# RWKV-7 scan on Trainium2: level products merged in pairs, state and masked products split over array quarters, second state decay on GpSimd

## What is computed

```python
def step(state, inp):
    r_t, w_t, k_t, v_t, kk_t, a_t = inp
    sa = jnp.einsum('bhvk,bhk->bhv', state, -kk_t)
    state = (state * w_t[:, :, None, :] + sa[..., None] * (kk_t * a_t)[:, :, None, :]
             + v_t[..., None] * k_t[:, :, None, :])
    return state, jnp.einsum('bhvk,bhk->bhv', state, r_t)
```

## Time and profile before

| | |
|---|---|
| Median of 3 runs | 2628.55 us (2627.21 to 2631.51) |
| The profiled execution's own time | 2627.98 us |
| Its span | 2626.2 us |
| Busy PE, DVE, ACT, POOL | 2399.8, 1562.1, 1080.5, 775.4 us |
| Mean granted clock | 0.968 |
| Matmul records | 22291 |

### The profile page before, as it was taken

The page is one execution under the profiler, slowest core; times in us unless marked ns, Lnnn a source line. Parts: engine busy times, 40 slices in busy tenths (PEclk is TensorE's granted clock), DMA queues, the critical chain, the costliest instruction groups (busy, mean ns, idle before and its releaser), DMA issues. The chain is left out here.

```text
span 2626.2 us, 53374 instructions
## 1 busy us (share of the span) xinstructions
PE 2399.8 (91%) x22291; PEld 1864.5 (71%) x22291; DVE 1562.1 (59%) x2402; ACT 1080.5 (41%) x1951; POOL 775.4 (30%) x511
## 2 busy tenths in 40 slices
PE   5799999999997899999989799998998996999997
PEld 2488887788886888888878666666876884555554
DVE  3544458976663445555377566666885886544433
ACT  4311123343442566656465455553122221544443
POOL 1122244545451455444213200001300000444443
PEclk8999999999998999999999999999998997999998
DMA  8522224344435123332044611104755446899994
GB/s 343 210 81 80 80 89 156 119 149 153 157 119 186 55 74 86 95 100 73 22 153 118 161 33 34 29 12 162 237 158 212 151 148 234 318 359 347 353 322 113
DMA packets 196291, 399.28 MB, mean 152 GB/s; under 512 B 38698, under 2 KB 104010, under 8 KB 182994
## 3 DMA queue, kind: packets, MB, share of 16 engines
q1 hardware_dynamic: 173876, 322.58, 36.2%
q0 software_dynamic: 12960, 41.82, 6.0%
q10 hardware_dynamic: 9216, 31.46, 3.0%
HBM read 294.57 MB, written 106.48 MB: 153 GB/s over the span
## 5 line engine op out<-in xcount | busy, mean ns | idle before, releaser
L99 PE MATMUL ps_in<-h_t_low,w_in_high 128*128 128x512 f32 x960 | 378.7, 394 | 2.1 <-PEq L79 2.1
L100 PE MATMUL ps_in<-h_t_high,w_in_low 128*128 128x512 f32 x960 | 373.9, 389 | 0.0
L101 PE MATMUL ps_in<-h_t_high,w_in_high 128*128 128x512 f32 x960 | 373.8, 389 | 0.0
L99 PEld LDWEIGHTS ps_in<-h_t_low,w_in_high 128*128 128x128 f32 x960 | 180.2, 188 | 44.5 <-issue 5.6
L1275 POOL TENSOR_TENSOR wkv_levels<-wkv_nt,level_mask 128x1024 f32<-128x1024 f32 x60 | 140.5, 2359 | 230.0 <-ACT wkv_nt L1220 230.0
L101 PEld LDWEIGHTS ps_in<-h_t_high,w_in_high 128*128 128x128 f32 x960 | 180.2, 188 | 38.0
L100 PEld LDWEIGHTS ps_in<-h_t_high,w_in_low 128*128 128x128 f32 x960 | 180.3, 188 | 35.7
L607 ACT COPY p_row<-ps_in 128x512 f32<-128x512 f32 x72 | 42.4, 588 | 293.4 <-PE ps_in L101 256.3
L3078 PE MATMUL ps_xy<-w_tile,hidden_turned 128*128 128x512 f32 x272 | 123.6, 597 | 16.4 <-DMA w_tile<-in_w 15.0
L498 POOL CAST w_in_high<-w_in_tile 128x1024 fp32r<-128x1024 f32 x39 | 45.7, 1171 | 299.3 <-PE ps_in L101 297.2
L705 DVE TENSOR_SCALAR p_mixed<-p_row,mu_centre 128x1537 f32<-128x1537 f32 x24 | 35.3, 1473 | 148.0 <-ACT p_row L607 147.8
(11 more groups left out here) (432 smaller groups left out, 6221.0 us busy)
## 6 DMA issues: line engine op xcount, KB each, us to landing
merged_t<-in_w SPq DMA_DIRECT2D x36, 1024.0 KB, 11.2
w_tile<-in_w SPq DMA_DIRECT2D x34, 1024.0 KB, 15.4
w_now<-in_w SPq DMA_DIRECT2D x30, 1024.0 KB, 15.8
w_ada_tile<-in_w_ada SPq DMA_DIRECT2D x12, 2048.0 KB, 9.2
wkv_in<-wkv_out SPq DMA_DIRECT2D x24, 1024.0 KB, 3.9
w_in_tile<-in_w_in SPq DMA_DIRECT2D x40, 512.0 KB, 3.6
p_t<-p_mixed ACTq DMA_DIRECT2D x24, 512.0 KB, 2.7
gates<-p_mixed ACTq DMA_DIRECT2D x16, 768.0 KB, 4.6
```

The source lines that it names most:

```text
L99: nc.tensor.matmul(out, w[0], x[1], start=start, stop=False)
L100: nc.tensor.matmul(out, w[1], x[0], start=False, stop=False)
L101: return nc.tensor.matmul(out, w[0], x[0], start=False, stop=stop)
```

## The change

1. `level_z` and `level_xz` make 16 products of 128 rows by 64 columns of weights with 64 moving columns, where they made 32 of 64 by 64 with 32. For this `x` gets a second copy of its shape: half `c` of the partitions holds values in place `c` and zeros in place 1 - c. `xt_over` becomes `xt_wide`, laid out likewise; ACT fills it with four copies of 64x256 (`widen`) instead of two, and reads it alone. `turned` makes two transposes of 64x512 instead of one of 128x512.
2. `from_state` and `mask_v` write each 128 columns as two products of 64 columns, `half(a)` of the weights to half `a` of the output: 32 products on four quarters instead of 16.
3. The PSUM tile `LV` has its axes exchanged, so that the first results of a level lie in one bank and the second in the other; `half_product` writes the second bank alone.
4. `decay_again` goes from ACT to POOL, as four operations of 128x256, ahead of `level(j + 2, 0)` in a pass. `next_state` is two operations of 128x256 on DVE, a wait for them, and one of 128x512.
5. Beta and kappa have two buffers instead of three: `load_bk(j + 3)` stands behind `load_ar(j + 3)` in SP's stream and waits for the turning of tile j + 1.

```diff
-        AR, BK, LB = 3, 3, 3
+        AR, BK, LB = 3, 2, 3
-        x = s.sb("wkv_x", [P, 2, 2 * H, BLK])
+        x = s.sb("wkv_x", [P, 2, 2, 2 * H, BLK])
-        xt_over = s.sb("wkv_xt_over", [P, H, BLK])
+        xt_wide = s.sb("wkv_xt_wide", [P, 2, 2, H, BLK])
...
-                if j + 3 < N:
-                    load_bk(j + 3)
...
                 if j + 3 < N:
                     load_ar(j + 3)
+                    load_bk(j + 3)
                 store(j, 1)
...
+                        for a in range(2):
+                            mm = nc.tensor.matmul(G[half(a), r, CH * hh(g, f):CH * hh(g, f) + CH], lbm[half(r), i % LB, 2 * d + c, slot(c, g, f), half(a)],
+                                                  uv[half(r), i % 2, c, d, 2 * f + g], start=True, stop=True)
...
-                for d, f, c, b in level_tiles:
+                for d, f, b in column_halves:
                     h = H * d + RF * b + f
-                    mm = nc.tensor.matmul(LV[half(b), c, 0, RF * d + f], lev[half(c), l, h], x[half(c), i % 2, h], start=True, stop=True)
+                    mm = nc.tensor.matmul(LV[half(b), 0, :, RF * d + f], lev[:, l, h], x[:, i % 2, :, h], start=True, stop=True)
...
-                for d, f, c, b in level_tiles:
-                    right = xt[half(c), i % 2, H * d + RF * b + f] if b == c else xt_over[half(b), RF * d + f]
-                    mm = nc.tensor.matmul(LV[half(c), b, 1, RF * d + f], z[half(b), c, RF * d + f], right, start=True, stop=True)
+                for d, f, c in column_halves:
+                    mm = nc.tensor.matmul(LV[half(c), 1, :, RF * d + f], z[:, c, RF * d + f], xt_wide[:, c, :, RF * d + f], start=True, stop=True)
...
-                    for g in range(2):
-                        mm = nc.tensor.matmul(Q[:, g, d, CH * f:CH * f + CH], ar[half(g), i % AR, d, f, pair(c)], s0[half(g), c, f],
+                    for g, a in quarters:
+                        mm = nc.tensor.matmul(Q[half(a), g, d, CH * f:CH * f + CH], ar[half(g), i % AR, d, f, pair(c)][:, half(a)], s0[half(g), c, f],
                                               start=(n == 0), stop=True, skip_group_check=True)
...
                 for b in range(2):
-                    ins = nc.scalar.copy(xt_over[half(b)].rearrange("p (d f) t -> p d (f t)", d=2), by_side(xt[half(1 - b), i % 2])[:, :, b])
+                    for c in range(2):
+                        ins = nc.scalar.copy(xt_wide[half(b), c, b].rearrange("p (d f) t -> p d (f t)", d=2), by_side(xt[half(c), i % 2])[:, :, b])
...
+                pool.wait_ge(m["s0_ready"], 2 * i + k + 1)
+                for d in range(2):
+                    c = chunk(k, d)
+                    ins = nc.gpsimd.tensor_tensor(s1[:, 1 - c], s0[:, c], decay(i, k, d).to_broadcast([P, RF, CH]), ALU.mult)
+                ins.then_inc(m["s1_ready"], 1)
...
             for j in range(-2, N):
+                if j >= 0:
+                    decay_again(j, 0)
+                    decay_again(j, 1)
                 if j + 2 < N:
                     level(j + 2, 0)
...
-                return nc.vector.transpose(flat(dst), flat(src))
+                for c in range(2):
+                    ins = nc.vector.transpose(flat(dst[half(c), c]), flat(src[half(c)]))
+                return ins
...
-                        for f in range(RF):
-                            ins = nc.vector.scalar_tensor_tensor(out=s0[:, 1 - c, f], in0=S[:, c, CH * f:CH * f + CH], scalar=decay(i, k, d, f),
-                                                                 in1=s1[:, 1 - c, f], op0=ALU.mult, op1=ALU.add)
-                    ins.then_inc(m["s0_ready"], 1)
+                        ins = nc.vector.tensor_tensor(s0[:, 1 - c], S[:, c].rearrange("p (f t) -> p f t", f=RF), decay(i, k, d).to_broadcast([P, RF, CH]), ALU.mult)
+                    ins.then_inc(m["s0_part"], 1)
+                    dve.wait_ge(m["s0_part"], 2 * i + k + 1 - int(i >= RUNS[1][0]))
+                    nc.vector.tensor_tensor(s0[:], s0[:], s1[:], ALU.add).then_inc(m["s0_ready"], 1)
...
+            for c in range(2):
+                nc.vector.memset(x[half(c), :, 1 - c], 0.0).then_inc(m["zeros"], 1)
+                nc.vector.memset(xt_wide[half(c), :, 1 - c], 0.0).then_inc(m["zeros"], 1)
```

60 lines of the change are left out of this document (27 added, 33 removed).

## The result

The changed kernel takes 2659.13 us (median of 4 runs, 2657.02 to 2659.66) against 2629.82 for the kernel before on the same chip: a ratio of 1.0111, 95% interval 1.0093 to 1.0128. The forecast was 2623, its range ended at 2640. The profiled execution took 2657.02 us, 29.04 more than that of before.

What follows compares the result with a forecast made beforehand. TensorE's program order was taken to bound the scan. 2627.98 us + 1 for the instructions - 7 for stalls + 1 for the lower clock = 2623 us, range 2609 to 2640.

Steps and rivals of the forecast that it cites:

- What bounds the kernel: Scan: TensorE's program order, 31.46 of a quiet tile's 33.94 us, with the other engines filling its shadow.
- the prices on TensorE: Scan: state and masked products from 1.93 to 1.07 us, level products 1.05, half_product's single bank uncharged; 3.44 saved a tile.
- (b): State and masked products: quarters do not overlap, groups stay at 1.93 or 1.98 us; 2642 us, chance 0.10.
- (e): Level products: 128-row weight loads do not overlap, 4.4 us a product group; 2950 us, chance 0.01.
- The helpers: VectorE's turns take 1.30 us, +0.59 five times a tile; ScalarE's widen 1.66, +0.84 four times.
- The walk: One scan tile in three stretches, ending at products, level_z(·,4), next second masked product: 34.1 us; together +1 without stalls.
- Rival (a): Scan: walk too kind to the helpers, joints between instructions cost; tile 34.8 us, 2638 us, chance 0.19.
- Two beta/kappa buffers: SP's load waits for an earlier turning, lands in 4.9 us, before its data are wanted; nothing charged.
- Stalls: Inside TensorE's groups: four tenths of the 17 us go, swallowed by its longer waits; -7 us.
- Rival (c): TensorE in the scan: fewer records also mean fewer stalls, 14 instead of 7 us go; 2612 us, chance 0.16.
- More idling brings the clock down more often: TensorE's clock in the scan: more time at the lower level, +1 us, between 0 and +8.
- State decay: POOL and VectorE in the scan: costs nothing as long as s1 is there; cover 0.2 us.

Runs made afterwards that it cites:

- e6: Kernel before with only two beta/kappa buffers and the load's new place: 2663.34 us, 1.0121 of the kernel before.
- e1: Changed kernel with the beta/kappa load issued later, behind the next pass's first level product: 2632.57 us, 0.9987 of the kernel before.
- e5: Kernel before with only the split state and masked products: 2658.82 us, 1.0103 of the kernel before.
- e3: Changed kernel without the merge of the level products (64x64 products, one transpose a turn, copy_over): 2667.68 us, 1.0125 of the kernel before.
- e11: Changed kernel with the late beta/kappa load and both masked products whole: 2624.83 us, 0.9969 of the kernel before.
- h4: Changed kernel with late beta/kappa load, only level_z merged, first masked product whole, 64 more records before the first tile: 2619.37 us, 0.9959 of the kernel before.
- e10: Kernel before with half of the alpha/rho load moved behind the next pass's first level product: 2621.77 us, 0.9959 of the kernel before.
- e7: Kernel before with only decay_again on POOL and next_state in three operations: 2634.53 us, 1.0016 of the kernel before.
- the four shifts: Four late-load variants of the changed kernel with 32, 64 or 96 more records before the first tile, tiles unchanged: 0.9959 to 1.0025 of the kernel before.
- h1: Changed kernel with late beta/kappa load, first masked product whole, 64 more records before the first tile: 2639.41 us, 1.0025 of the kernel before.
- h3: Changed kernel with late beta/kappa load, only level_z merged, first masked product whole, 32 more records before the first tile: 2637.49 us, 1.0022 of the kernel before.
- f2: Changed kernel with late beta/kappa load, only level_z merged, first masked product whole, half of alpha/rho late too: 2636.07 us, 0.9982 of the kernel before.
- f4: Kernel before, three buffers, with beta/kappa and half of alpha/rho loaded behind the next pass's first level product: 2635.06 us, 0.9984 of the kernel before.

## Why the prediction failed, step by step

**What bounds the kernel; the prices on TensorE.** Right. State and masked products take 1.09 (forecast 1.07), level products 1.08 (1.05), so rivals (b) and (e) are out. The merged products' records follow each other 34 ns apart. `half_product` writes one bank in 0.68 us, as `cross_product` does.

**The helpers.** Right in size but for one addition. Timeline of DVE, changed kernel, end of one tile and beginning of the next:

```profile
1120.05 2.25 DVE L1376 TENSOR_TENSOR wkv_state_decayed<-wkv_state_decayed,wkv_state_decayed_twice 128x512 f32<-128x512 f32 x1
...
1136.52 1.43 DVE L1322 STREAM_TRANSPOSE wkv_x<-wkv_xt 64x512 f32<-64x512 f32 x2
```

Timelines of ACT, then of POOL, in the later of the two tiles:

```profile
1129.59 1.64 ACT L1185 COPY wkv_xt_wide<-wkv_xt 64x256 f32<-64x256 f32 x4
```

```profile
1137.09 1.23 POOL L1266 TENSOR_TENSOR wkv_state_decayed_twice<-wkv_state_decayed,p_end 128x256 f32<-128x256 f32 x2
```

A turn 1.43 (forecast 1.30), `widen` 1.64 (1.66), POOL's pair 1.23 (1.4), `next_state` 0.76 + 0.69 (1.6). The addition in the first row takes 2.25, of which more below. The state product that needs its result starts at 1132.13, ten microseconds after its end, so here it costs nothing.

**The walk.** Right: 34.3 us without stalls against 34.1. Stretch 1 took 12.0 (12.3), stretch 2 14.29 (13.9), stretch 3 8.08 (7.9). Rival (a) asked for 34.6 or more and did not come. So +1 us for the instructions themselves was sound, and the other 28 are elsewhere.

**"Two beta/kappa buffers: ... its data are wanted ... such a load lands in 4.9 us".** This is the step that failed. It asked whether the load comes in time, and it does. It did not ask what the load does while it lands. Before, it was issued in the middle of a pass; now it is issued beside the store at the end, so that masked, cross and level products run 5 to 8 us behind it. e6 prices the move alone at +1.2%, e1 its undoing at -1.2%. What it does shows in the packets: TensorE's next block of instructions starts behind the load's first 512 KB, up to 4.2 us after the border before instead of 1.2. The store behind it, which I had looked at, kept no engine waiting. The step isn't the only one that failed: e5 loses 1.0% with every load in its old place, and that belongs to the next term.

**"Stalls ... I take four tenths of the 17 us as gone: -7".** The second failed step, wrong in sign: +13.3. I had treated the stalls as evenly strewn, so that more waiting would swallow them. They stand at block borders, worst behind a load and where 128 records take less than the 3.3 to 3.9 us from one block to the next. The split put 128 more records into a tile, 96 of them into the seam between two passes, which was dense already. Rival (c) had the one half of it that is true, that fewer records mean fewer stalls: e3 against the changed kernel, 63.5 to 29.6. The other half, that the split undoes this at its place, is e5 (58.5).

**"More idling brings the clock down more often: +1, between 0 and +8".** Mis-sized: 27.3 us more at the lower clock, some 12 us of time by the estimate above. With next to no stalls (e11) the eleven tiles run at 1.00. But the lower clock doesn't go by the sum of the stalls: h4 has 30.2 us of short ones and none of it, e10 14.3 us and 44.4 of it. What brings it down is not shown here.

**State decay: nothing.** Right (e7).

**What would show it.** The last mark that I had named, a lower clock for more than twice the time now, came true in the eleven tiles (47.8 us against 20.5), though not over the whole scan (65 against 39); I had not said which. A mark for the stalls themselves was missing.

**What stays open.** That TensorE stalls at the borders of its instruction blocks is shown by the counts, the four shifts and the packets, and so is that a load delays a block. Open is when TensorE asks for one. After a wait of TensorE the packet can start before the border before is reached, up to 0.9 us in the changed kernel, and a dense block there passes without a stall; I have no rule that forecasts this, and mine failed in h1, h3 and h4. Open too is what brings the clock down.

## What to carry to other kernels

Price a bulk load's place, not only its arrival: ask what TensorE issues 5 to 8 us after it, and try it where TensorE waits anyway (it paid in e1, and not in f2 and f4). Count a design's records as well as its group times: a group that is faster because it is cut into more records can lose the gain to stalls at the instruction blocks' borders, and one merge that saves no time can pay by its records. And before a difference of half a per cent is put down to an edit, shift the stream by a few dozen records and measure again: here 32 records more or less moved a kernel between 0.996 and 1.002 on one chip.
